# Second attention's tail reordered, and its low-rank gate computed from x in plain fp32 in four groups of 32 output partitions

## The chip, the cores and the metric

One core of a Trainium2 chip runs the kernel. The metric is the device time of one execution in microseconds (us); less is better. The core has a matrix engine (TensorE, PE in the profile), three engines for vectors (VectorE or DVE, ScalarE or ACT, GpSimd or POOL) and SyncE (SP), which only issues DMAs here. Each runs its own stream of instructions in order; they meet through semaphores.

## The reference, cut to what matters

The whole is two layers of chunked attention and retention, then a feed-forward block, a token mixer, a second feed-forward block and a norm, for 512 tokens of width 1024 in fp32. The change lies in the token mixer alone. Its input `u` is the normalised activation, and the projection `p = u @ w_in` is split into a pool part, the first linear attention ("hgrn"), the rwkv part, and the second linear attention ("gla"):

```python
gq, gk, gv, gg, ga = jnp.split(p_gla, [G, 2 * G, 3 * G, 4 * G], axis=-1)      # G = 256, ga is 16 wide
log_a = jax.nn.log_sigmoid(ga @ gla_w2 + gla_b) / GLA_GATE_TAU
o_g = chunked_gated_linear_attention(split_heads(gq * QK_SCALE), split_heads(gk),
                                     split_heads(gv), split_heads(log_a))
o_g = (o_g * lax.rsqrt(jnp.mean(o_g * o_g, axis=-1, keepdims=True) + NORM_EPS)).reshape(B, T, G)
y_gla = o_g * gla_norm * jax.nn.silu(gg)
```

The rwkv part is a recurrence over tokens with a decay `exp(-exp(w_log))`, `a = sigmoid(rwkv_a0 + xa @ rwkv_a2)`, keys normalised per head, `kk = kk / max(sqrt(sum(kk * kk)), 1e-12)`, and a gate `g_r = sigmoid(xg) @ rwkv_g2`.

## The kernel before, in words

Everything is written out by hand, one instruction stream per engine; each wait is on a named signal, and `of(name, key)` gives the value of the semaphore that the named instruction raised. The same Python loops stand in the stream of each engine, so a step `n` on one engine answers to step `n` on the others.

A weight unit is a tile of 128x1024. SyncE loads it, ScalarE rounds it to its high part (`w_high`), VectorE subtracts to get the low part (`w_low`), and TensorE multiplies 8 k tiles with three passes each (high x high, high x low, low x high: 24 matmuls of 512 columns, `three_passes`). `use()` on ScalarE and VectorE splits the next unit, three units ahead. TensorE's results land in eight PSUM banks, taken in turn by `take(key, freed_by)`: it waits until what lay in that bank has been read by the instruction named at its last take. So a product can wait for a reader of eight takes ago that has nothing to do with it.

The token mixer runs in this order. Pool and hgrn projections; then `linear_attention("hgrn")`; then `linear_attention("gla")`; then `inverse` (the rwkv chunks' triangular matrices are inverted by doubling, sizes 2 to 32); then `recurrence` with the output product as its filler. A linear attention walks over nine sizes, `ORDER = (32, 16, 8, 4, 2, 1, 64, 128, 256)`. Step n is: VectorE makes the logs of the decays (`logs`), ScalarE their exponentials (`factor`), VectorE the products with keys and queries (`factors`, tile `E`), TensorE the score products (`scores`, L862 for sizes up to 64, L873 for 128, L876 for 256), and VectorE copies those (`near`, L1644) or ScalarE does (`far`). In front of the scores of each step a `fill(n + 1)` puts other work: in hgrn the four value units of hgrn, the five units "gla a", "gla q" and "gla k", then two value units of gla; in gla the other two value units and the eight rwkv projections, and from step 6 on `operand_steps`, which prepares the rwkv operands (decays, key norms, gates).

"gla a" is the low-rank gate: before, its 16 columns are padded to a unit of their own (128 output columns, three passes over the normed input `xg`), scaled by VectorE into 16 rows of `ga`, and multiplied with `gla_w2` over these 16 rows ("gla gate", 2 products of 512 columns).

What the names of the later steps stand for: "rwkv landed" (tile `shifted`) is VectorE's scaled copy of a projection, "rwkv own" ScalarE's and "rwkv mixed" VectorE's mix with the token before. "key floored" is a tiny VectorE step, "key inverse" GpSimd's power of -0.5, "key spread" ScalarE's copy of it over the key tile, "key turned" TensorE's transposes of that, "key scaled" VectorE's product. "sigma" and "a gate" are ScalarE's sigmoids of low-rank products ("sigma in", "a gate in"), "sigma summed" VectorE's scans. "mixed" is the last product of a linear attention (40 pairs of 128x64 blocks), in two halves; the second half needs "far" of size 256. `finish` norms and gates its result. `keep_busy(n)` multiplies n times 512 columns that nobody reads.

## Time and profile before

| | us |
|---|---|
| median of 3 runs | 1684.16 (1682.77 to 1685.19) |
| the profiled execution | 1687.16 |
| its span in the profile | 1685.2 |

| engine | busy us | share |
|---|---|---|
| PE (TensorE matmuls) | 1650.3 | 98% |
| DVE (VectorE) | 861.3 | 51% |
| ACT (ScalarE) | 669.0 | 40% |
| POOL (GpSimd) | 124.7 | 7% |

The mixer's part from the start of `linear_attention("hgrn")` to the end of `inverse` is about us 989 to 1235 of the span. The page's row of the granted clock of TensorE cuts the span into 40 slices of 42 us; slices 27 to 30 cover 1138 to 1264. A matmul's duration in a timeline runs until its result has landed, and the next one starts before that, so the pace of a stream is read from starts, not from durations.

### The profile page before, as it was taken

The page shows a single profiled execution, that of the slowest core. Times are in us where ns is not written, and L with a number is a line of the kernel's source. Part 1 is how long each engine was busy: PE and PEld are TensorE (multiplying, and loading weights), DVE is VectorE, ACT ScalarE, POOL GpSimd, SP SyncE. Part 2 cuts the span into 40 slices and gives each one's busy share as a digit, 9 for nine tenths or more (in the row PEclk, how much of TensorE's full clock was granted, in tenths as well). Part 3 has the DMA queues.
Part 4 walks back from the last instruction along what each step waited for, and adds up shares of the span by engine and source line. Part 5 has one row for each costly group of instructions (what it writes and reads, how often), then busy time and mean ns, then how long its engine had stood idle before and what let it go on. Part 6 is the DMA issues. An engine that isn't in the chain of part 4 may idle for free.

```text
span 1685.2 us, 23809 instructions
## 1 busy us (share of the span) xinstructions
PE 1650.3 (98%) x9540; PEld 1338.2 (79%) x9540; DVE 861.3 (51%) x1170; ACT 669.0 (40%) x1017; POOL 124.7 (7%) x126
## 2 busy tenths in 40 slices
PE   9999999999999999999999999998999999999997
PEld 6877778877777888888888878887877888888886
DVE  6733445542444565444433478577556554444333
ACT  6145565314656433233222355346333433333221
POOL 0001001000100110000000310000410200000000
PEclk9999999999999999999999999997899999999999
DMA  5412212331221223332233422220002232232331
GB/s 180 154 63 76 88 51 88 113 125 63 75 77 53 98 85 103 100 101 90 88 103 94 141 76 63 63 66 18 3 23 86 88 101 92 96 97 85 103 98 56
DMA packets 40750, 144.14 MB, mean 86 GB/s; under 512 B 4816, under 2 KB 4832, under 8 KB 40256
## 3 DMA queue, kind: packets, MB, share of 16 engines
q1 hardware_dynamic: 37296, 131.61, 24.7%
q0 software_dynamic: 2192, 8.87, 1.6%
q10 hardware_dynamic: 1152, 2.14, 0.4%
q8 instruction: 76, 1.25, 0.3%
q14 instruction: 34, 0.28, 0.1%
...
## 4 chain that ended last, share of the span: by engine, by line
PE 85%; DVE 8%; ACT 5%; issue 1%; POOL 0%; DMA 0%; DVEq 0%; ACTq 0%; SPq 0%; POOLq 0%
PE bank L497 25%; PE bank L499 24%; PE bank L498 24%; PE bank L479 3%; PE bank L1017 2%; PE bank L485 1%; DVE sb_w_low L1230 1%; PE bank L664 1%; PE bank L728 1%; PE bank L707 1%; ACT sb_w_high L1999 1%; DVE sb_E L1230 1%; PE bank L862 1%; DVE sb_near L1644 1%; DMA sb_x<-xT 0%
## 5 line engine op out<-in xcount | busy, mean ns | idle before, releaser
L1230 DVE TENSOR_TENSOR sb_w_low<-sb_raw,sb_w_high 128x1024 fp32r<-128x1024 f32 (+1 forms) x253 | 310.9, 1229 | 368.0 <-ACT sb_w_high L1999 361.5
L497 PE MATMUL bank<-sb_xg_high,sb_w_high 128*128 128x512 f32 x1176 | 465.6, 396 | 2.0 <-DVE sb_w_low L1230 1.4
L499 PE MATMUL bank<-sb_xg_high,sb_w_low 128*128 128x512 f32 x1176 | 459.0, 390 | 0.0
L498 PE MATMUL bank<-sb_xg_low,sb_w_high 128*128 128x512 f32 x1176 | 458.5, 390 | 0.0
L1999 ACT ACTIVATE sb_w_high<-sb_raw 128x1024 fp32r<-128x1024 f32 (+1 forms) x253 | 263.3, 1041 | 349.1 <-PE bank L499 325.1
L497 PEld LDWEIGHTS bank<-sb_xg_high,sb_w_high 128*128 128x128 f32 x1176 | 221.1, 188 | 65.3 <-issue 15.8
L499 PEld LDWEIGHTS bank<-sb_xg_high,sb_w_low 128*128 128x128 f32 x1176 | 221.0, 188 | 47.1
L498 PEld LDWEIGHTS bank<-sb_xg_low,sb_w_high 128*128 128x128 f32 x1176 | 221.3, 188 | 44.3 <-issue 0.2
L499 PE MATMUL bank<-sb_h_high,sb_w_low 128*128 128x512 f32 x352 | 136.9, 389 | 0.0
L497 PE MATMUL bank<-sb_h_high,sb_w_high 128*128 128x512 f32 x352 | 136.9, 389 | 0.0
L498 PE MATMUL bank<-sb_h_low,sb_w_high 128*128 128x512 f32 x352 | 136.9, 389 | 0.0
L497 PE MATMUL bank<-sb_w_high,sb_xg_high 128*128 128x512 f32 x256 | 103.2, 403 | 0.0
L498 PE MATMUL bank<-sb_w_low,sb_xg_high 128*128 128x512 f32 x256 | 100.3, 392 | 0.0
L499 PE MATMUL bank<-sb_w_high,sb_xg_low 128*128 128x512 f32 x256 | 100.0, 391 | 0.0
L2586 POOL TENSOR_TENSOR sb_square_sum<-sb_square_sum,sb_square 128x512 f32<-128x512 f32 x20 | 26.1, 1307 | 748.4 <-ACT sb_square L1999 748.4
L499 PEld LDWEIGHTS bank<-sb_h_high,sb_w_low 128*128 128x128 f32 x352 | 66.1, 188 | 13.8
L498 PEld LDWEIGHTS bank<-sb_h_low,sb_w_high 128*128 128x128 f32 x352 | 66.1, 188 | 13.8
L497 PEld LDWEIGHTS bank<-sb_h_high,sb_w_high 128*128 128x128 f32 x352 | 66.1, 188 | 13.5
L1999 ACT ACTIVATE sb_h_high<-sb_up 128x512 fp32r<-128x512 f32 x44 | 27.8, 632 | 115.8 <-DVE sb_up L1230 115.8
L1230 DVE TENSOR_TENSOR sb_up<-bank,sb_inv_rms 128x512 f32<-128x512 f32 x44 | 30.4, 691 | 78.2 <-PE bank L499 77.4
L1999 ACT ACTIVATE sb_gate<-sb_gate 128x512 f32<-128x512 f32 x44 | 27.8, 632 | 92.3 <-DVE sb_gate L1230 92.3
L497 PEld LDWEIGHTS bank<-sb_w_high,sb_xg_high 128*128 128x128 f32 x256 | 48.3, 189 | 17.1 <-issue 7.1
...
## 6 DMA issues: line engine op xcount, KB each, us to landing
...
```

The lines of the kernel that those rows point to most:

```text
L479: made = e.matmul(out, lhsT, rhs, start=n == 0, stop=n == len(pairs) - 1)
L485: made = e.transpose(banks[i][:, blk(n)], in_, mem.ident)
L497: e.matmul(out, w[0], v[0], start=first, stop=False)
L498: e.matmul(out, w[0], v[1], start=False, stop=False)
L499: return e.matmul(out, w[1], v[0], start=False, stop=last)
L664: made = e.matmul(out[k], m.feat["rk"][r, f, blk(j)], m.feat["rq"][r, f, j * P:], start=part == 0, stop=part == 1)
L707: e.matmul(out[k], m.qT[r, j, blk(q)], m.kT[r, j, 0:keys], start=True, stop=True).then_inc(*p.up("scores", n, 2 * j + k, q))
L728: made = e.matmul(out[64 * k:64 * k + 64, blk(q)], m.tok["av"][:, key, h * ATT_DIM:(h + 1) * ATT_DIM], m.probT[:, 2 * (q % 2) + k, blk(key ...
L1017: made = e.matmul(out(banks[i], t, c), left(t, c), right(t, c), start=True, stop=True)
L1230: e.tensor_tensor(out, a, b, op).then_inc(*v.up(*signal))
L1999: e.activation(out, in_, func, bias=bias, scale=scale, accum_out=accum).then_inc(*a.up(*signal))
L2586: e.tensor_tensor(out, a, b, op).then_inc(*g.up(*signal))
```

## The change

- Low-rank gate: no weight unit any more. GpSimd scales a small table `gla_w` (128 x 8 x 32, 16 columns and 16 zeros per k tile) by the norm's gain; TensorE multiplies it with `x` itself in plain fp32, k tile k into output partitions 32 (k mod 4) to 32 (k mod 4) + 31 of one bank, 8 matmuls of 512 columns. VectorE scales all 128 rows. The second product runs over 128 rows: `gla_w2` is repeated four times with zero rows between, so it sums the four partial results. This stands in the same step as "gla q" 0, the second product in the step after.
- The hgrn part's fills: one more value unit of gla takes the place of the "gla a" unit, and the gla part has one fewer.
- gla's tail: "key squares" go to a tile of their own (`key_sq`, in the room of `y_rwkv`) and to step 3, "rwkv tanh" to step 4, the gla gate's silu (`bend_gate`) to step 2 ahead of the projection's ScalarE work. `operand_steps` is cut anew; "sigma before" and its exponential go away, since `kkE` is made from the fades `eB` shifted by one token within a chunk.
- Between gla and `inverse`: "X preset" and "XT preset" are signalled per head and stand beside the two halves of "mixed"; `rE` is made after the first masks of `inverse`; gla's `finish` is cut in two, the second half behind the updates of size 2.

```diff
@@ TensorE
                 if name == "gla" and n == len(ORDER) - 1:
-                    keep_busy(3)
+                    fill(len(ORDER))
+                    keep_busy(2)
                 scores(n)
-            if name == "gla":
-                keep_busy(1)
-            fill(len(ORDER))
+            if name == "hgrn":
+                fill(len(ORDER))
...
         def gla_steps():
-            projected("gla a", 0, "gla a landed")
-            yield
-            for f in range(2):
-                i = take(("gla gate", f), ("gla sized", f))
-                p.wait_ge(*of("gla a landed"))
-                group(banks[i][:, :], [(m.gla_w2[0:16, blk(f)], m.ga[0:16, :])], "gla gate", f)
+            i = take(("gla a",), ("gla a landed",))
+            p.wait_ge(*of("gla weights"))
+            for k in range(KT):
+                r = slice(k % 4 * 32, k % 4 * 32 + 32)
+                made = e.matmul(banks[i][r, :], m.gla_w[:, k, :], x[:, k, :], start=k < 4, stop=k >= 4)
+            made.then_inc(*p.up("gla a"))
             for f in range(2):
                 projected("gla q", f, "gla q landed", f)
                 yield
+                if f == 0:
+                    for part in range(2):
+                        i = take(("gla gate", part), ("gla sized", part))
+                        p.wait_ge(*of("gla a landed"))
+                        group(banks[i][:, :], [(m.gla_w2[:, blk(part)], m.ga)], "gla gate", part)
                 projected("gla k", f, "gla k landed", f)
...
-                next(values_h if n < 3 else others if n < 8 else values_g)
+                next(values_h if n < 3 else others if n < 7 else values_g)
...
         def operand_steps():
-            yield
             for f in range(2):
                 for what, r in (("sigma", slice(0, 64)), ("a gate", slice(64, 128))):
...
-                    group(banks[i][:, at:at + 2], [(m.kI[:, f, blk(t)], mem.table("same_head")[:, 0:P:64])], "key norm")
+                    group(banks[i][:, at:at + 2], [(m.key_sq[:, f, blk(t)], mem.table("same_head")[:, 0:P:64])], "key norm")
+            yield
+            yield
+            for f in range(2):
+                i = take(("key turned", f), ("key scaled", f))
+                p.wait_ge(*of("key spread"))
+                transposes(i, [flat(m.key_sq)[:, blk(2 * t + f)] for t in range(TT)], "key turned", f)
...
             yield
             for half in range(2):
                 i = take(("gate out", half), ("g tok", half))
                 for j in range(2):
                     group(banks[i][:, j * G:(j + 1) * G], [(m.mixed[:, 7, blk(2 * half + j)], m.lora[:, 1, :])],
                           "gate out", half)
...
-            for f in range(2):
-                i = take(("key turned", f), ("key scaled", f))
-                p.wait_ge(*of("key spread"))
-                transposes(i, [flat(m.kI)[:, blk(2 * t + f)] for t in range(TT)], "key turned", f)
-            yield
-            yield
             yield
 
...
         def fill_gla(n):
             if n < 2:
-                next(values_g)
+                if n == 0:
+                    next(values_g)
                 next(projections)
@@ VectorE
                     ALU.mult, ALU.add, "rwkv mixed", f)
                 yield
 
-        rr, rk, kk, eI = m.mixed[:, 0:2, :], m.mixed[:, 2:4, :], m.bI, m.rE
+        rr, rk, kk, eI = m.mixed[:, 0:2, :], m.mixed[:, 2:4, :], m.kI, m.rE
 
         def operand_steps():
-            yield
             norms = small[:, 176:192]
             v.wait_ge(*of("key norm"))
             ts(norms, bank("key norm")[:, 0:16], 1e-24, None, ALU.max, ALU.bypass, "key floored")
             yield
-            v.wait_ge(*of("sigma", 1))
-            for f in range(2):
-                scan(m.cum[:, f, :], m.sigma[:, f, :], "sigma summed", f)
-            tt(m.tmp, m.cum, m.sigma, ALU.subtract, "sigma before")
             for f in range(2):
                 v.wait_ge(*of("key turned", f))
                 stt(kk[:, f, :], rk[:, f, :], mem.col("rwkv_k_k", f), bank("key turned", f)[:, :], ALU.mult, ALU.mult,
                     "key scaled", f)
             yield
-
+            for f in range(2):
+                v.wait_ge(*of("sigma", f))
+                scan(m.cum[:, f, :], m.sigma[:, f, :], "sigma summed", f)
+            yield
             v.wait_ge(*of("a gate", 1))
-            v.wait_ge(*of("rwkv exps"))
-            tt(m.kkE, kk, m.tmp, ALU.mult, *STEP)
             tt(m.bI, kk, m.a_gate, ALU.mult, *STEP)
-            stt(m.bI, m.bI, -1.0, eI, ALU.mult, ALU.mult, *STEP)
-            yield
             for f in range(2):
 
                 ts(m.tmp[:, f, :], m.a_gate[:, f, :], 1.0, mem.col("rwkv_k_a", f), ALU.subtract, ALU.mult, *STEP)
                 stt(rk[:, f, :], m.tmp[:, f, :], 1.0, rk[:, f, :], ALU.add, ALU.mult, *STEP)
 
-                stt(m.sigma[:, f, :], rr[:, f, :], mem.col("rwkv_r_k", f), rk[:, f, :], ALU.mult, ALU.mult, *STEP)
-            yield
-            tt(m.kI, rk, eI, ALU.mult, *STEP)
+                stt(m.sigma[:, f, :], rr[:, f, :], mem.col("rwkv_r_k", f), rk[:, f, :], ALU.mult, ALU.mult,
+                    "bonus products")
             v.wait_ge(*of("rwkv fades"))
-            tt(m.rE, rr, m.eB, ALU.mult, "rE")
+            stt(m.bI, m.bI, -1.0, eI, ALU.mult, ALU.mult, *STEP)
+            by_chunk = lambda ap: flat(ap).rearrange("p (n c) -> p n c", c=CHUNK)
+            out, keys, fades = by_chunk(m.kkE), by_chunk(kk), by_chunk(m.eB)
+            ts(out[:, :, 0:1], keys[:, :, 0:1], 1.0, None, ALU.mult, ALU.bypass, *STEP)
+            tt(out[:, :, 1:], keys[:, :, 1:], fades[:, :, 0:CHUNK - 1], ALU.mult, "kkE")
+            tt(m.kI, rk, eI, ALU.mult, "kI")
             yield
 
         projections, operand_prep = rwkv_steps(), operand_steps()
 
         def fill_gla(n):
             if n < 6:
-                if n < 2:
+                if n == 0:
                     next(values_g)
-                if n == 0:
-                    finish_hgrn()
+                    for _ in finish_hgrn():
+                        pass
                 next(projections)
                 if n in (2, 4):
...
                     next(projections)
             e.copy_predicated(chunks(ap), over_tiles(mask).bitcast(I32),
                               chunks(bank(what, h)[:, 0:TT * CHUNK])).then_inc(*v.up(*signal))
 
-        v.wait_ge(*of("X preset"))
-        v.wait_ge(*of("XT preset"))
         for h in HEADS:
             masked("AT", m.AT[:, h, :], h, mem.table("before"))
+            v.wait_ge(*of("XT preset", h))
             first_pairs("AT", m.XT[:, h, :], h, mem.chunk_pairs(1), "XT made", 2, h)
+            v.wait_ge(*of("X preset", h))
             first_pairs("X", m.X[:, h, :], h, mem.table("pairs_ts"), "X made", 2, h)
-        finish_gla()
+        tt(m.rE, m.mixed[:, 0:2, :], m.eB, ALU.mult, "rE")
+        finishing = finish_gla()
+        next(finishing)
 
...
                     update("X", m.X[:, h, :], False, h)
                 update("XT", m.XT[:, h, :], True, h)
+            if size == 2:
+                next(finishing)
             next(side, None)
@@ ScalarE
             for half in range(2):
                 a.wait_ge(*of("mixed", name, half))
+                if name == "gla" and half:
+                    preset("XT", m.XT)
                 act(m.y_tok[name][:, 2 * half:2 * half + 2, :], groups_of(bank("mixed", name, half)[:, :], G),
                     "mixed landed", name, half, scale=0.125 if name == "hgrn" else 1.0)
+                if name == "gla" and not half:
+                    a.wait_ge(*of("factors read", "gla", len(ORDER) - 1))
+                    preset("X", m.X)
...
+        def key_squares():
+            a.wait_ge(*of("rwkv mixed", 3))
+            for f in range(2):
+                act(m.key_sq[:, f, :], m.mixed[:, 2 + f, :], "key squares", func=ACT.Square, scale=mem.col("rwkv_k_k", f))
+
+        def low_rank_tanh():
+            a.wait_ge(*of("rwkv mixed", 6))
+            act(m.mixed[0:64, 6, :], m.mixed[0:64, 6, :], "rwkv tanh", func=ACT.Tanh)
+
         def operand_steps():
+            yield
+            a.wait_ge(*of("key inverse"))
+            act(heads(flat(m.key_sq)), small[:, 176:192].unsqueeze(2).to_broadcast([P, 16, 64]), "key spread")
             a.wait_ge(*of("rwkv mixed", 7))
-            act(m.mixed[0:64, 6, :], m.mixed[0:64, 6, :], "rwkv tanh", func=ACT.Tanh)
             a.wait_ge(*of("xg read", MIX_NORM))
-            for f in range(2):
-                act(m.kI[:, f, :], m.mixed[:, 2 + f, :], "key squares", func=ACT.Square, scale=mem.col("rwkv_k_k", f))
-            yield
             for f in range(2):
                 for what, out, bias in (("sigma", m.sigma, "rwkv_w0"), ("a gate", m.a_gate, "rwkv_a0")):
                     a.wait_ge(*of(what + " in", f))
                     act(out[:, f, :], bank(what, f)[:, :], what, f, func=ACT.Sigmoid, bias=mem.col(bias, f))
             act(m.mixed[:, 7, :], m.mixed[:, 7, :], "rwkv sigmoid", func=ACT.Sigmoid)
-            a.wait_ge(*of("key norm"))
-            a.wait_ge(*of("key inverse"))
-            act(heads(flat(m.kI)), small[:, 176:192].unsqueeze(2).to_broadcast([P, 16, 64]), "key spread")
+            act(small[:, 250:251], mem.ones[:, 0:1], *STEP, func=ACT.Exp)
             yield
+            yield
+            a.wait_ge(*of("sigma summed", 1))
+            act(m.rE, m.cum, "rwkv exps", func=ACT.Exp, scale=HALF_E)
+            act(m.eB, m.cum, "rwkv fades", func=ACT.Exp, scale=-HALF_E)
             for half in range(2):
                 a.wait_ge(*of("gate out", half))
                 act(m.g_tok[:, 2 * half:2 * half + 2, :], groups_of(bank("gate out", half)[:, :], G),
                     "g tok", half)
             yield
-            a.wait_ge(*of("sigma before"))
-            act(m.tmp, m.tmp, *STEP, func=ACT.Exp, scale=-HALF_E)
-            act(m.rE, m.cum, "rwkv exps", func=ACT.Exp, scale=HALF_E)
-            act(m.eB, m.cum, "rwkv fades", func=ACT.Exp, scale=-HALF_E)
-            yield
-            yield
...
         def fill_gla(n):
             if n < 2:
-                next(values_g)
                 if n == 0:
+                    next(values_g)
                     finish_hgrn()
                 next(projections)
             elif n < 6:
+                if n == 2:
+                    bend_gate("gla")
                 next(projections)
                 if n in (2, 4):
                     next(projections)
+                if n == 3:
+                    key_squares()
+                elif n == 4:
+                    low_rank_tanh()
             else:
                 next(operand_prep)
-            if n == 4:
-                bend_gate("gla")
...
             pass
-        preset("X", m.X, "factors read")
-        preset("XT", m.XT, "mixed")
         inverse(m, finish_gla)
...
                 act(out[:, i, :], bank(name, i)[:, :], name, i)
         a.wait_ge(*of("bonus in"))
         act(mem.small[:, 112:128], bank("bonus")[:, 0:16], "bonus")
-        finish_gla()
@@ GpSimd
+        g.wait_ge(s.loads("mixer tables"), 16 * 6)
+        tt(m.gla_w, m.gla_w, mem.columns(GAINS[MIX_NORM]).unsqueeze(2).to_broadcast([P, KT, 32]), ALU.mult,
+           "gla weights")
```

Left out are the room for the new tables, the same `fill_gla` on VectorE and ScalarE, and the renamed signals. Unchanged are ScalarE's "Gv" copies in `inverse`, which wait for "y made" of gla (the end of `finish`) and stand ahead of size 4's "Pm" copies, and GpSimd's `gate_steps`, whose first step behind size 2 waits for the same signal.

## Rows read from the trace of the kernel before

**Rows 1.** Windows: stretch, length, busy PE, PEld, DVE, ACT, POOL, clock, DMA share, GB/s.
```profile
1120.00:1135.00 15.00, 15.00 (x90) 12.43 (x89) 12.31 (x16) 6.54 (x7) 0.00 (x0) 1.00 0.17 52
...
1157.00:1166.00 9.00, 9.00 (x51) 7.89 (x50) 4.39 (x7) 6.99 (x10) 3.44 (x1) 0.53 0.01 2
```
**Rows 2.** Timeline of PE: start, length, what, shapes, count; plain fp32 counts two each.
```profile
1130.03 0.39 PE L499 MATMUL bank<-sb_xg_high,sb_w_low 128*128 128x512 f32 x1
1135.47 0.39 PE L499 MATMUL bank<-sb_xg_high,sb_w_low 128*128 128x512 f32 x1
...
1019.77 1.98 PE L479 MATMUL bank<-sb_ga,sb_gla_w 16*128 16x512 f32 x4
...
472.87 1.09 PE L728 MATMUL bank<-sb_probT,sb_av 128*64 128x128 f32 x16
```
**Rows 3.** Windows, just behind the second low-rank product.
```profile
1022.00:1024.00 2.00, 2.00 (x6) 1.53 (x5) 1.86 (x3) 0.43 (x1) 0.00 (x0) 0.54 0.00 0
```
**Rows 4.** Timeline of PE, the score products of two steps behind it.
```profile
1028.98 2.00 PE L862 MATMUL bank<-sb_E 64*128 64x64 f32 x32
1036.59 2.00 PE L862 MATMUL bank<-sb_E 64*128 64x64 f32 x32
```
**Rows 5.** Timeline of DVE in the gla part; in brackets idle time before, and what ended it.
```profile
1103.00 1.23 DVE L1230 TENSOR_TENSOR sb_w_low<-sb_raw,sb_w_high 128x1024 fp32r<-128x1024 f32 x1 [2.72 <-ACT sb_w_high L1999]
...
1124.47 0.69 DVE L1230 TENSOR_TENSOR sb_shifted<-bank,sb_inv_rms 128x512 f32<-128x512 f32 x1
...
1132.50 0.69 DVE L1230 TENSOR_TENSOR sb_shifted<-bank,sb_inv_rms 128x512 f32<-128x512 f32 x1
...
1142.29 1.53 DVE L1230 TENSOR_TENSOR sb_E<-sb_E,sb_kq_gla 128x1024 f32<-128x1024 f32 x1 [1.05 <-ACT sb_E L1999]
...
1144.99 0.69 DVE L1230 TENSOR_TENSOR sb_shifted<-bank,sb_inv_rms 128x512 f32<-128x512 f32 x1
```
**Rows 6.** Timeline of ACT in the gla part: value landings, a table load, the silu.
```profile
1098.97 2.85 ACT L1999 ACTIVATE sb_v_gla<-bank,sb_inv_rms_t 128x512 f32<-128x512 f32 x4
...
1137.47 1.28 ACT L1999 ACT_TABLE_LOAD   x1
1138.77 1.06 ACT L1999 ACTIVATE sb_v_gla<-sb_v_gla 128x1024 f32<-128x1024 f32 x1
```
**Rows 7.** Timelines of POOL, PE, DVE and ACT in gla's tail.
```profile
1157.88 3.44 POOL L2586 TENSOR_TENSOR sb_small<-sb_small 128x16 f32<-128x16 f32 x1 [182.54 <-DVE sb_small L1234]
...
1157.42 3.68 PE L862 MATMUL bank<-sb_E 64*128 64x64 f32 x32
...
1166.48 2.48 DVE L1250 TENSOR_TENSOR_SCAN sb_cum<-sb_mixer,sb_sigma 128x512 f32<-128x512 f32 x2
...
1161.40 1.05 ACT L1999 ACTIVATE sb_kI<-sb_small 128x1024 f32<-128x1024 f32 x1 [1.49 <-POOL sb_small L2586]
...
1165.21 1.29 ACT L1999 ACTIVATE sb_g_tok<-bank 128x512 f32<-128x512 f32 x2
...
1173.58 2.66 ACT L1999 ACTIVATE sb_far<-bank 128x512 f32<-128x512 f32 x4
...
1176.93 0.60 ACT L1999 ACTIVATE sb_y_gla<-bank 128x512 f32<-128x512 f32 x1 [0.69 <-PE bank L479]
```
**Rows 8.** Timelines of PE, DVE and POOL in the first sizes of the inverse.
```profile
1183.08 0.69 PE L1008 MATMUL bank<-sb_kkE,sb_bI 64*64 64x64 f32 x32
...
1187.46 0.42 DVE L1230 TENSOR_TENSOR sb_AT<-bank,sb_mixer 128x256 f32<-128x256 f32 x1 [4.57 <-ACT sb_XT L1999]
...
1196.95 1.06 PE L1017 MATMUL bank<-sb_Pm,sb_XT 64*64 64x32 f32 x16 [2.62 <-ACT sb_Pm L1999]
...
1199.40 0.29 DVE L1230 TENSOR_TENSOR sb_X<-sb_X,bank 128x128 f32<-128x128 f32 x1
...
1207.90 0.66 PE L1017 MATMUL bank<-sb_X,sb_CT 64*64 64x64 f32 x16
...
1203.33 2.69 POOL L2586 TENSOR_TENSOR sb_offset<-sb_tokB,sb_small 128x256 f32<-128x256 f32 x4 [0.17 <-POOL sb_CT L2586]
```

62 lines of the change are left out of this document (34 added, 28 removed).

## The prediction

> **What bounds the kernel now.** I read the page first: TensorE is busy for 98% of the span, and the row of its granted clock is full everywhere but in two slices, both in the token mixer. So the change can only pay in the mixer. Then the windows of that stretch. Up to 1143 TensorE is busy without a gap while VectorE is at 12.31 of 15 us [rows 1]: TensorE sets the pace there, with VectorE close behind. In gla's tail the clock is at its lower level (1.2 GHz): 0.53 over 1157 to 1166 [rows 1]; it fell behind the last projections, where TensorE had to wait for ScalarE's tanh. In the tail no engine is full. There a chain through all four engines decides, so I read the timelines of each engine there and followed each wait by hand. The same goes for the first sizes of the inverse, where TensorE waits 2.62 us for a copy by ScalarE and VectorE starts 4.57 us late behind "XT preset" [rows 8].
>
> All clock times below are on the scale of the trace of before. A shift of the path counts one to one on the end, because from size 4 of the inverse on the waits keep their order.
>
> **Part 1, the low-rank gate.** A weight unit takes 5.44 us of TensorE from the first to the 25th start [rows 2]. The new product is 8 plain fp32 matmuls of 512 columns. Its price one after the other comes from the second product: 2 such matmuls took 1.98 us [rows 2], four passes with a landing of 0.16 in it, so one costs 0.86 (a 512-column pass 0.43), and eight cost 6.9. But matmuls that write different groups of output partitions overlap: 8 matmuls of 128 columns into two groups of 64 took 1.09 us with the last one's landing of some 0.2 in it, where one after the other they take 8 x 0.43 / 2 = 1.72 [rows 2]. That is 0.11 each, a factor of 2 for two groups. Four groups I take at a factor of 4: 1.7 us and a landing, 1.9. The ends are 1.7 and, without any overlap, 6.9; a factor of 2 gives 3.4. The value taken is nearest to the row with groups.
>
> The Trainium skill, TensorE: Matmul & The Clock Gate, section "Measured speedup vs the span model", has three groups of 32 columns at 2.38 times, not 3. At that share four groups would give 3.2 times, an estimate of 2.2 us, and the sum below would be 0.3 higher. No row here has four groups of 32.
>
> The second product stays at two matmuls of 512 columns and 1.98 us. But behind it the clock is at 0.54 [rows 3], and the projection that follows takes from 1021.75 to the scores at 1028.98, 7.2 us, where between other steps it is 36.59 - 28.98 - 2.0 = 5.6 [rows 4]. This product used 16 rows, the idle array being the only thing that sets it apart. With 128 rows I expect the clock to stay: -1.6 us, between 0 and -1.6.
>
> One value unit takes the freed step, so the hgrn part keeps its count of units and ends 1.9 - 1.6 = **0.3 us later**. VectorE has little to do while the hgrn part's last product runs, so this shift goes on as it is. GpSimd's scaling of the table and the sixth table load are done some 25 us before TensorE asks; if not, the gap would show before "gla a".
>
> **Part 2, the gla part has one unit fewer.** TensorE saves 5.44 us, but it no longer sets the pace. VectorE's landings of two projections that have one step between them are 1132.50 - 1124.47 = 8.03 us apart [rows 5], of which 0.8 is a wait on ScalarE; TensorE needs 5.6 + 2.0 = 7.6. So VectorE's own work decides from the first landing to the last, at 1144.99 [rows 5]. Along VectorE:
> - The gla values land (2.85 us on ScalarE [rows 6]) now ahead of the root that hgrn's `finish` waits for, and VectorE's landing 0 stands behind that: +2.9 (bounds +2.5 to +3.0).
> - The removed step saves its wait and its split, 2.72 + 1.23 [rows 5], with 0.1 of issue: -4.0.
> - The silu in step 2 stands ahead of the split's first half on ScalarE: 1.28 + 1.06 [rows 6] and the 1.06 of that half, less 1.7 that VectorE has to do meanwhile: +1.7. Its old place cost 1.05 [rows 5] and a slower product, 1.53 in place of 1.23: -1.3. The squares and the tanh fit into ScalarE's waits: 0.
>
> Sum: -0.7. With part 1 the last landing comes at 1144.99 - 0.7 + 0.3 = 1144.6, **0.4 us earlier**. TensorE is done with its projections some 7 us before that: nearly the whole saved unit turns into idle time of TensorE.
>
> **Part 3, the tail.** "key floored" came at 1157.6, just before GpSimd's power of 3.44 us [rows 7]. It moves one step ahead: about 1152.0. Power to 1155.5, key spread (1.05 [rows 7]) to 1156.6, table load 1.28 [rows 6], sigma read at 1158.7. Here a bank decides: between its take for sigma 0 and its second take for the scores of size 64 TensorE takes eight, so these scores wait for ScalarE's sigma, which now stands behind the power, the spread and the table load. They start at 1158.7 instead of 1157.42 [rows 7]. They run on the lower clock, since TensorE stood idle before: 3.68 us [rows 7], to 1162.4. The transposes behind them end their first half at 1163.2, and "key scaled" begins, 7 us earlier than before (1170.3). VectorE waits from 1157.7 to 1163.2 for that. Behind it on VectorE are queued two keys, 1.6; the logs, copies and product of sizes 256 and 64, 4.4; the scans, 2.48 [rows 7] and issue: scans done at 1171.8, before 1166.48 + 2.48 = 1169.0. ScalarE: two exponentials, 2.2, then "g tok", 1.29 [rows 7], which stood ahead of the scans before, then "far", 2.66 [rows 7]: to 1178.2, where before it ended at 1176.24. The second half of "mixed" needs it and runs 1183.08 - 1176.93 = 6.15 us [rows 7, 8]. The inverse starts at 1184.4 instead of 1183.08: **+1.3**. VectorE is ready at 1181, 2 us before it was; that gain has no taker. Bounds: full clock on scores and transposes -2.5; `keep_busy` and gate product still on the lower clock when "far" is done +1.5.
>
> **Part 4, the inverse.** Let I be its start. VectorE's first mask waits for the last landing (fence), which stands behind XT preset: I + 2.6 instead of I + 4.4. That alone gains nothing, as the second pair of heads is bound by TensorE: masks end at I + 10.5 in both. Then rE, squares and sum, 3 x 1.25, instead of all of `finish`, 5.6: first update at I + 14.4, before I + 16.3 [rows 8]. ScalarE's "Pm" loses the root ahead of it: I + 12.1 instead of 1196.95 - 1183.08 = I + 13.9 [rows 8]. But the second half of `finish` (2.7 us) ends at I + 21.3, where it was at I + 16.2. On it wait ScalarE's "Gv", with size 4's "Pm" queued behind, and GpSimd's four products of 2.69 us [rows 8], with the next "below" mask (0.73) behind. TensorE's third product of size 4 needs that mask: I + 25.0, before 1207.90 - 1183.08 = I + 24.8 [rows 8]. So the head start of 1.8 is lost again: **+0.2**, between -1.7 (if TensorE keeps its clock in the transposes and VectorE's masks follow) and +3.4.
>
> **Sum.** Hgrn part +0.3, gla part -0.7, from the last landing to the start of the inverse 39.8 us instead of 38.1, which is +1.7, inverse +0.2: **+1.5**. The profiled execution took 1687.16 (span 1685.2), so it would take 1688.7; it stands 3.0 above the median of the runs, 1684.16, and against that the sum gives **1685.7**. Its own bounds, from the -2.5, +1.5, -1.7 and +3.4 above, of which no two should come in full together: 1682.5 to 1689.
>
> **Rivals.**
> A. TensorE's saving arrives whole: VectorE is not the bound in the gla part. For it: TensorE without a gap up to 1143 [rows 1]. Against: the step of 8.03 against 7.6 [rows 5, 4]. It gives -5.4 - 1.6 + 1.9 = -5.1: 1679.0.
> B. The clock holds in the tail, as sigma, norm and scores now follow the projections closer. Against: some 5 us of waiting before the scores of size 1 and again before those of size 64. It gives -2.5 in the tail and -1.5 in the inverse on top of the forecast: 1681.7.
> C. Slower: the clock falls in the inverse. TensorE waits from I + 19.3 to I + 22.7 for "Pm" behind "y made"; before, the idle time of 2.62 us [rows 8] was followed by a stretch on the lower clock. One stretch of lower clock costs about 1.7, as behind the second low-rank product (7.2 us in place of 5.6 [rows 4]), two cost 3.4. It decides if the new wait is as long as the old one. It gives 1687.4 to 1689.1; I take 1688.5.
> D. The four groups don't overlap (or two at a time): +5.0 (+1.5), since the hgrn part is bound by TensorE: 1690.7 (1687.2).
>
> **How the numbers follow.** Forecast 0.36, A 0.22, B 0.11, C 0.24, D 0.07. The measurement can tell a change of about 0.2%, 3.4 us: faster is below 1680.8, slower above 1687.5. Faster: A and a little of B, 0.23. Slower: C and D, and a little of the forecast's upper edge, 0.32. Same: 0.45. The range takes in A and D's far end: 1678.5 to 1691.0; the forecast's own is 1682.5 to 1689.
>
> **What would show it.** "gla a" as 16 rows of plain fp32 within 2 us, starts in fours; no window under 1.00 behind the second product; VectorE's last landing of a projection near 1144.6, with TensorE done by 1138; scores of size 64 starting right behind ScalarE's first sigma; "far" ending near 1178; "Gv" on ScalarE waiting for y_gla. I am wrong if VectorE waits for TensorE in the gla part, if the scores of size 64 start before sigma is read, or if "mixed" runs through without a stop.

## The result and the profile after

The changed kernel takes **1696.42 us** (median of 9 executions, 1688.46 to 1700.32), the kernel before 1686.78 beside it (9 executions, 1682.77 to 1690.96): a ratio of 1.0056, 95% interval 1.0041 to 1.0072. It is slower by 9.6 us. The forecast was 1685.7, within 1678.5 to 1691.0.

The executions of the changed kernel are of two sorts that differ in TensorE's mean granted clock: 1688.5 and 1690.2 us at 0.987, and seven between 1695.2 and 1700.3 at 0.982 to 0.984. The one with the profile is the fastest of the nine, 1688.46 (span 1686.6). Against the profiled execution of before, 1687.16, the difference is only 1.3. So this profile doesn't show one of the executions that make the median, and that has to be kept in mind in all that is read from it.

The page of the changed kernel, its span, TensorE's busy time and its clock by fortieths of the span:

```profile
span 1686.6 us, 23786 instructions
PE 1640.1 (97%) x9528; PEld 1329.2 (79%) x9528; DVE 860.0 (51%) x1169; ACT 667.3 (40%) x1016; POOL 126.5 (7%) x128
...
PEclk9999999999999999999999999996999999999998
```

The row shows the low clock in one fortieth, where gla's tail lies (the 8 in the last place is the end of the kernel). Stretches of a few us are too short to show in it.

**The low-rank gate.** The timeline of PE of the changed kernel in the hgrn part: the new product, the second product, the scores of the step behind it, which answer to [rows 2] and [rows 4]:

```profile
1011.25 1.92 PE L922 MATMUL bank<-sb_x,sb_gla_w 128*32 128x512 f32 x16
...
1020.70 1.98 PE L481 MATMUL bank<-sb_ga,sb_gla_w 128*128 128x512 f32 x4
...
1028.10 2.00 PE L864 MATMUL bank<-sb_E 64*128 64x64 f32 x32
```

Eight fp32 matmuls (16 records) in four groups take 1.92 us. Behind the second product the scores start at 1028.10, which is 5.4 us after its end in place of 7.2, and the clock stays up.

**The gla part.** VectorE's last landing of a projection, then its longest waits from 1103 to 1144, by engine and total, and in a last fence TensorE's in the same stretch to 1145:

```profile
1143.88 0.69 DVE L1239 TENSOR_TENSOR sb_shifted<-bank,sb_inv_rms 128x512 f32<-128x512 f32 x1
```

```profile
DVE sb_mixed L1247 <- ACT sb_mixed L2013: 4.8, 6, 0.8
DVE sb_w_low L1239 <- ACT sb_w_high L2013: 2.4, 3, 1.8
```

```profile
PE bank L499 <- DVE sb_w_low L1239: 0.6, 1, 0.6
```

VectorE never waits for TensorE there. TensorE, which had no gap in this stretch before, now waits 0.6 us for VectorE.

**The tail.** Timelines of DVE, POOL, ACT and PE, in that order, from the floored norms to the inverse's first product; they answer to [rows 7]:

```profile
1151.02 0.17 DVE L1243 TENSOR_SCALAR sb_small<-bank 128x16 f32<-128x16 f32 x1
...
1162.78 1.60 DVE L1247 SCALAR_TENSOR_TENSOR sb_kI<-sb_mixed,sb_cols,bank 128x512 f32<-128x512 f32 x2 [6.00 <-PE bank L487]
...
1168.87 2.55 DVE L1259 TENSOR_TENSOR_SCAN sb_cum<-sb_mixer,sb_sigma 128x512 f32<-128x512 f32 x2
...
1151.27 3.44 POOL L2608 TENSOR_TENSOR sb_small<-sb_small 128x16 f32<-128x16 f32 x1 [175.12 <-DVE sb_small L1243]
...
1157.19 0.69 ACT L2013 ACTIVATE sb_sigma<-bank,sb_cols 128x512 f32<-128x512 f32 x1
...
1171.45 1.06 ACT L2013 ACTIVATE sb_rE<-sb_cum 128x1024 f32<-128x1024 f32 x1 [2.32 <-DVE sb_cum L1259]
1172.54 1.06 ACT L2013 ACTIVATE sb_eB<-sb_cum 128x1024 f32<-128x1024 f32 x1
1173.69 1.29 ACT L2013 ACTIVATE sb_g_tok<-bank 128x512 f32<-128x512 f32 x2
1175.07 2.66 ACT L2013 ACTIVATE sb_far<-bank 128x512 f32<-128x512 f32 x4
...
1158.02 3.68 PE L864 MATMUL bank<-sb_E 64*128 64x64 f32 x32 [5.96 <-ACT sb_sigma L2013]
...
1170.30 3.20 PE L815 MATMUL bank<-sb_inv_rms,sb_ones 128*128 128x512 f32 x4
1173.43 2.00 PE L878 MATMUL bank<-sb_E 64*128 64x256 f32 x16
...
1184.43 0.69 PE L1015 MATMUL bank<-sb_kkE,sb_bI 64*64 64x64 f32 x32
```

Read it along the forecast's chain: the bank wait of the scores of size 64 on sigma (5.96 us), the low clock on them (3.68), the wait of "key scaled" (6.00), the scans, the exponentials and "g tok" ahead of far, far's end at 1177.73, the inverse at 1184.43. Each is there.

**The inverse.** Timelines of PE and ACT around size 4, which answer to [rows 8]:

```profile
1194.88 0.66 PE L1024 MATMUL bank<-sb_Pm,sb_XT 64*64 64x32 f32 x16 [0.71 <-ACT sb_Pm L2013]
...
1206.22 0.66 PE L1024 MATMUL bank<-sb_Pm,sb_XT 64*64 64x32 f32 x16 [3.45 <-ACT sb_Pm L2013]
...
1208.43 1.12 PE L1024 MATMUL bank<-sb_X,sb_CT 64*64 64x64 f32 x16 [0.97 <-POOL sb_CT L2608]
...
1204.83 0.86 ACT L2013 ACTIVATE sb_Gv<-bank 128x256 f32<-128x256 f32 x2 [4.92 <-DVE sb_y_gla L1239]
```

The wait of 2.62 us at size 2 [rows 8] has become 0.71, and a new one of 3.45 stands at size 4, behind "Gv", which waits for "y made". Behind it the clock is at its lower level for 6.8 us (from 1207.1 on).

Where do the other 8 us of the median go? That took other kernels, some of whose traces fell into executions of the second sort.

### The profile page after: what moved, and what is told of

It is laid out like the page before. It is cut to its first block, busy times and chain, and to the rows that moved or that the text cites. A ratio compares the mean times of both kernels' runs of the same rounds, so it can differ in the third digit from the quotient of the medians.

```text
span 1686.6 us, 23786 instructions
## 1 busy us (share of the span) xinstructions
PE 1640.1 (97%) x9528; PEld 1329.2 (79%) x9528; DVE 860.0 (51%) x1169; ACT 667.3 (40%) x1016; POOL 126.5 (7%) x128
## 4 chain that ended last, share of the span: by engine, by line
PE 86%; DVE 7%; ACT 4%; issue 1%; POOL 1%; DMA 0%; DVEq 0%; ACTq 0%; SPq 0%; POOLq 0%
PE bank L499 25%; PE bank L501 24%; PE bank L500 24%; PE bank L481 3%; PE bank L487 2%; PE bank L1024 1%; PE bank L666 1%; PE bank L730 1%; DVE sb_w_low L1239 1%; PE bank L709 1%; DVE sb_E L1239 1%; ACT sb_w_high L2013 1%; PE bank L864 1%; DVE sb_near L1653 0%; DMA sb_x<-xT 0%
```

## The experiments

In all of them the kernel before ran beside on the same chip; ratios are to it. The experiments are called e1 to e17, in the order in which they were made, not in that of the text. "At 0.983" is the mean granted clock of an execution. "The faster sort" and "the slower sort" are the two groups of executions above; a stretch is time that TensorE spends at 1.2 GHz without a break. Lengths and places of stretches are from the traces' record of the granted clock, and a trace shows one execution of its kernel.

### Again, and by halves

The changed kernel once more, no edit (e1):

> The changed kernel unchanged. Its nine runs fall into two groups: 1688.5 and 1690.2 us at a mean granted clock of 0.987, and 1695.2 to 1700.3 at 0.982 to 0.984, and the one execution with a trace is of the fast group. Theory K (clock): the path itself costs only +1 to +3 us, as in that trace, and most executions have further stretches at the lower clock, some 0.004 x 1690 x 2 = 13 us of them, at a place that the trace so far does not show. Then the times split in two groups again, and a trace of the slower group would show extra windows below 1.00 between the second attention and the inverse. Theory P (path): the new order of the tail waits longer in every execution, by 8 to 10 us, and the traced one was an exception; then times lie evenly between 1688 and 1700 and a trace shows later waits at full clock.

Measured: 1695.23 us (7 executions), ratio 1.0047 (1.0028 to 1.0067). Again two sorts: 1688.47, 1690.8 and 1692.05 at 0.987, four from 1695.23 to 1700.05 at 0.982 or 0.983. With the first nine that makes 5 executions of the faster sort and 11 of the slower. The trace was again of the faster sort.

Only the gate (e2: the diff's parts on `w_mix_ga`, `gla_w`, `gla_w2`, the `gla_steps` of the three engines and the fills that go with them; tail and inverse of before):

> Only the low-rank gate is changed (plain fp32 product in four groups, second product over 128 rows, one weight unit less, and the steps that move up with it); the tail and the inverse are those of before. My steps give for it: hgrn part +0.3, gla part about -0.7 to -1.3 because VectorE sets the pace, so the same as before within 1 us (ratio 0.999 to 1.000). Theory K leaves the place of the lost clock open: if it hangs on the idle time of TensorE after the projections, which this part alone makes longer, this kernel shows 1695 too. Theory P puts all of the loss in the tail, so this kernel is not slower than before (1684 to 1687).

Measured: 1685.68, ratio 1.0001 (0.9991 to 1.0010), mean clocks 0.986 to 0.990. The gate costs nothing and brings nothing that can be measured, as I had written.

Only tail and inverse (e3: the rest of the diff):

> Only the tail and the inverse are reordered; the low-rank gate is a full weight unit as before. My steps give +1.7 in the tail and +0.2 in the inverse: about 1688 to 1690 us, ratio 1.001 to 1.002, against 1686.8 before. Theory P: the whole loss is here, 1695 to 1697 (ratio 1.005 to 1.006). Theory K: in two groups by clock, or in the lower one alone if the clock is lost to the idle time that the gate part adds.

Measured: 1697.47, ratio 1.0057 (1.0038 to 1.0076); five of six executions at 0.982 to 0.984, one, 1690.95, at 0.986. The whole loss is in the tail and the inverse. This trace is of the slower sort (1696.89). The timeline of PE between the halves of 'mixed', then two windows:

```profile
1179.33 0.41 PE L480 MATMUL bank<-sb_v_gla,sb_near 128*128 128x64 f32 x2 [1.15 <-ACT sb_far L2007]
```

```profile
1178.00:1185.00 7.00, 5.85 (x38) 5.74 (x38) 4.12 (x5) 3.36 (x7) 0.00 (x0) 0.76 0.01 2
1185.00:1198.00 13.00, 13.00 (x116) 12.63 (x116) 2.63 (x6) 3.56 (x8) 1.45 (x2) 0.50 0.00 1
```

TensorE stands for 1.15 us between the halves of 'mixed', and from 1181.6 on the clock is at 1.2 GHz for 17.1 us. That covers most of the second half of 'mixed', the first products of the inverse (L1008) and its transposes; TensorE is busy without a gap in the second of the windows. The same windows of the changed kernel's own trace, where there is no such wait:

```profile
1178.00:1185.00 7.00, 7.00 (x91) 6.92 (x89) 2.77 (x4) 2.69 (x7) 0.00 (x0) 1.00 0.01 2
1185.00:1198.00 13.00, 11.94 (x304) 11.15 (x298) 9.63 (x16) 8.01 (x17) 5.18 (x6) 1.00 0.01 3
```

In 13 us, 304 matmuls against 116.

`finish` put back ahead of the first updates (e4; ScalarE's part of it goes back too, which the cut below doesn't show):

```diff
-        finishing = finish_gla()
-        next(finishing)
+        for _ in finish_gla():
+            pass
...
-            if size == 2:
-                next(finishing)
```

> The changed kernel with the second half of the last normalization (reciprocal, scaling, gate) put back ahead of the inverse's first updates on VectorE, and its root back ahead of the first copies on ScalarE, as before the change. My steps: the first update comes 1.8 us later, and the wait for Pm behind 'y made' is gone: -0.2 +- 1.5. Rival C (the clock falls in the inverse while TensorE waits behind 'y made'): this takes the cause away, so the two groups of times become one near 1687 to 1689, and windows from 1205 to 1215 us are back at 1.00.

Measured: 1692.93, ratio 1.0042 (1.0027 to 1.0058); six executions at 1688.7 to 1691.6 (0.986, 0.987), six at 1694.3 to 1701.2 (0.979 to 0.983). So the wait behind "y made" is not what parts the two sorts, and my rival C is not the missing loss. The second thing that I had written, full clock from 1205 to 1215, did not come either: there are 6.8 us at 1.2 GHz from 1204.8 on. Its trace is of the slower sort:

```profile
1170.64 1.88 PE L815 MATMUL bank<-sb_inv_rms,sb_ones 128*128 128x512 f32 x4
1172.46 2.00 PE L878 MATMUL bank<-sb_E 64*128 64x256 f32 x16
...
1178.23 0.41 PE L481 MATMUL bank<-sb_v_gla,sb_near 128*128 128x64 f32 x2 [0.96 <-ACT sb_far L2011]
```

```profile
1187.95 1.13 PE L1015 MATMUL bank<-sb_kkE,sb_bI 64*64 64x64 f32 x32
...
1200.94 0.27 PE L1024 MATMUL bank<-sb_X,sb_CT 64*64 64x64 f32 x2 [0.38 <-DVE sb_XT L1843]
```

```profile
1175.43 2.66 ACT L2011 ACTIVATE sb_far<-bank 128x512 f32<-128x512 f32 x4
```

Compare the changed kernel's trace. There the stretch at 1.2 GHz in the tail lasts 27.3 us, to 1172.9, the two fillers of `keep_busy(2)` take 3.20, and the scores behind them start at 1173.43. Here it lasts 23.9, to 1170.6, the fillers take 1.88, and the scores start at 1172.46. Far ends at the same time in both, 1177.7 and 1178.1, because ScalarE, not TensorE, sets it. So TensorE, 1 us earlier thanks to the better clock, gets 1 us to wait, and then the clock falls for 17.1 us. The inverse starts at 1187.95 in place of 1184.43.

### More and less of the wait

One filler between the halves (e5):

```diff
+                if name == "gla" and half:
+                    keep_busy(1)
                 i = take(("mixed", name, half), ("mixed landed", name, half))
```

> The changed kernel with one fp32 filler matmul of 512 columns (0.86 us at full clock) between the two halves of the last 'mixed'. In the two traces of the slower group TensorE stood still for 1.0 us at that place, waiting for ScalarE's last far copy, and the clock fell 2.7 to 3.4 us later, for 17.1 us, over the second half of 'mixed' and the start of the inverse; in the trace of the faster group the half-clock stretch before it was one slice longer, the filler ahead of it took 3.4 instead of 1.9 us, 'mixed' began 1 us later and ran through. Theory W (that wait decides): now it runs through in every execution; all times 1688 to 1690 at 0.987. Theory S (how long the earlier half-clock stretch was decides, whatever stands in 'mixed'): two groups as before, median 1695 to 1696.

Measured: 1691.37, ratio 1.0045 (1.0027 to 1.0063); eight executions at 1688.1 to 1691.9 (0.986 to 0.989), three at 1699.6 to 1701.3 (0.983). Three stayed slow, so neither forecast came out as written. In the trace, which is of the faster sort, 0.19 us of the wait is left, and the next stretch at 1.2 GHz lasts 3.4 us, from 1187.2:

```profile
1178.02 0.41 PE L481 MATMUL bank<-sb_v_gla,sb_near 128*128 128x64 f32 x2 [0.19 <-ACT sb_far L2015]
```

The fillers ahead of the last scores taken out (e6):

```diff
                     fill(len(ORDER))
-                    keep_busy(2)
```

> The changed kernel without its two filler matmuls ahead of the scores of the last size. 'mixed' then begins 1.9 us earlier, and far comes at the same time, so TensorE waits 2 to 3 us between the halves in place of 0 to 1. Theory W: all executions are of the slower group, 1695 to 1700 at 0.981 to 0.983. Theory S: the two groups stay, about one in three at 1688. Fillers that only delay: 1 us faster.

Measured: 1698.83, ratio 1.0081 (1.0068 to 1.0093); all five executions at 0.980 to 0.982. Work was left out and it became slower:

```profile
1177.82 0.69 PE L481 MATMUL bank<-sb_v_gla,sb_near 128*128 128x64 f32 x2 [2.77 <-ACT sb_far L2012]
```

The other way round, the kernel **before** given such a wait (e10):

```diff
+            for _ in range(2):
+                act(m.eB, m.cum, *STEP, func=ACT.Exp, scale=-HALF_E)
             act(m.eB, m.cum, "rwkv fades", func=ACT.Exp, scale=-HALF_E)
```

> The kernel before with ScalarE's exponential 'rwkv fades' made three times over in place of once: 2.1 us more ahead of the last far copies, so far ends near 1178.3 as in the changed kernel in place of 1176.2, and TensorE waits about 1.0 us between the halves of 'mixed'. Nothing else is changed. Theory W: that wait alone moves most executions to a mean clock of 0.983 to 0.985 with a stretch of some 17 us from 1181 on; median 1693 to 1697. By the path alone: +1.0, 1687.

Measured: 1693.00, ratio 1.0047 (1.0035 to 1.0059); all five at 0.982 to 0.984. The wait is 1.58 us, and 20.5 us at 1.2 GHz follow from 1179.4 on, where before has 3.4:

```profile
1178.88 0.43 PE L479 MATMUL bank<-sb_v_gla,sb_near 128*128 128x64 f32 x2 [1.58 <-ACT sb_far L1999]
```

One window over 'mixed' and the start of the inverse, of this kernel, then of before:

```profile
1174.00:1206.00 32.00, 28.45 (x290) 26.87 (x288) 16.48 (x25) 15.20 (x26) 3.41 (x4) 0.68 0.00 1
```

```profile
1174.00:1206.00 32.00, 29.16 (x521) 28.18 (x520) 22.08 (x37) 14.87 (x30) 7.63 (x10) 0.84 0.01 2
```

Two superfluous instructions on ScalarE, 2.1 us, cost 6.9 in all. No part of the change is in this kernel, and nothing was added to or taken from TensorE's work: only the wait is new. That is most of the loss, rebuilt.

"g tok" ahead of the exponentials, so that far comes earlier (e9):

```diff
-            a.wait_ge(*of("sigma summed", 1))
-            act(m.rE, m.cum, "rwkv exps", func=ACT.Exp, scale=HALF_E)
-            act(m.eB, m.cum, "rwkv fades", func=ACT.Exp, scale=-HALF_E)
             for half in range(2):
                 a.wait_ge(*of("gate out", half))
...
+            a.wait_ge(*of("sigma summed", 1))
+            act(m.rE, m.cum, "rwkv exps", func=ACT.Exp, scale=HALF_E)
+            act(m.eB, m.cum, "rwkv fades", func=ACT.Exp, scale=-HALF_E)
```

> The changed kernel with ScalarE's two copies 'g tok' put ahead of the two exponentials of the summed sigma, into the 2.3 us in which ScalarE waits for the scans; before, they stand behind the exponentials and ahead of the last far copies, which end at 1178.2. Theory W (a wait of about 1 us between the halves of 'mixed' lowers the clock): far ends 0.7 to 1.3 us earlier, by 1177, the second half runs through as in the kernel before (far at 1176.2, half at 1177.3), and nearly all executions are at 0.987 or above: 1686 to 1689. By the path alone, without the clock: at most -1 on each of the two groups, median 1694 to 1696.

Measured: 1691.38, ratio 1.0038 (1.0019 to 1.0056); six executions at 1685.8 to 1689.0 (0.987, 0.988), six at 1693.7 to 1700.1 (0.980 to 0.985). The faster ones are 2 to 3 us better than the changed kernel's, but half are still of the slower sort: a miss. The trace, which is of that sort, shows why:

```profile
1173.54 2.66 ACT L2013 ACTIVATE sb_far<-bank 128x512 f32<-128x512 f32 x4
```

```profile
1176.35 0.41 PE L481 MATMUL bank<-sb_v_gla,sb_near 128*128 128x64 f32 x2 [1.32 <-ACT sb_far L2013]
```

Far ends at 1176.2 as foreseen. But here the tail's stretch at 1.2 GHz lasted only 17.1 us, TensorE did the gate product at full clock and was early by still more, and the wait is 1.32.

The same with three fillers in the inverse's wait (e11):

```diff
+            if size == 2:
+                keep_busy(3)
             next(side, None)
```

> As e9, and three filler matmuls (2.6 us at full clock) in the wait of 3.45 us in which TensorE stands for Pm behind 'y made' at the inverse's size 4. If idle time is what lowers the clock there, the stretch of 6.8 us from 1207 on goes, and it is 1.5 to 3 us faster than e9: 1684 to 1687. If the filler takes a bank that is not free, or the clock falls all the same: 0 to +3 on e9.

Measured: 1697.01, ratio 1.0057 (1.0039 to 1.0074); 1685.87 and 1688.29 at 0.989, four from 1696.7 to 1697.6 at 0.984. Which sort an execution falls into is chance here, so the median of six says nothing on the filler; e15 against e14, further down, does. Its trace says something on the two sorts: up to 'mixed' this kernel is e9, word for word, but in this execution the tail's stretch lasted 23.9 us, not 17.1; TensorE came later, there is no wait between the halves, and the execution took 1685.87.

### Fillers elsewhere

Fillers in the tail's two long waits, and the one of e5 between the halves (e7; the cut shows the first two):

```diff
+                if name == "gla" and ORDER[n] in (1, 64):
+                    keep_busy(5 if ORDER[n] == 1 else 7)
```

> As the kernel with the filler between the halves of 'mixed', and fillers too in the two long waits of the tail: five matmuls (4.3 us at full clock) ahead of the scores of size 1, where TensorE stands still for 4.2 us, and seven (6.0 us) ahead of those of size 64, where it stands still for 6.0. If the idle time of TensorE is what lowers the clock, the stretch of 24 to 27 us from 1146 on goes; scores and transposes of the tail take half as long (3.7 to 1.9 us each), and the inverse starts about 1.5 to 3 us earlier: 1683 to 1687. If the fill does not keep the clock, it adds its own time, 1 to 5 us, to the changed kernel's.

Measured: 1697.09, ratio 1.0074 (1.0060 to 1.0089), at mean clocks of 0.987 to 0.990. The trace is of the slowest of the six executions, 1704.18; the others took 1695.89 to 1698.06. In it the tail's stretch has shrunk from 27.3 us to 6.8, and it cost all the same:

```profile
1146.06 4.56 PE L815 MATMUL bank<-sb_inv_rms,sb_ones 128*128 128x512 f32 x10 [0.39 <-DVE sb_shifted L1243]
1151.17 2.00 PE L864 MATMUL bank<-sb_E 64*128 64x64 f32 x32 [0.55 <-DVE sb_near L1657]
1159.37 7.68 PE L815 MATMUL bank<-sb_inv_rms,sb_ones 128*128 128x512 f32 x14 [6.20 <-ACT sb_sigma L2017]
```

The first filler works: the scores of size 1 take 2.00 us in place of 3.68. The second takes a bank that sigma's reader still holds, so it waits 6.20 us itself and then stands for 7.7 us ahead of the scores that it should have helped. A filler needs a bank as any product does. Between the halves 1.78 us of waiting are left in this trace, and 20.5 us at 1.2 GHz follow from 1186.1 on, so the kernel has lost in both ways; how much of the time goes to which was not measured.

The kernel before with four fillers ahead of the sigma products and one between the halves (e8; `keep_busy(4)` behind the first `yield` of TensorE's `operand_steps`):

> The kernel before with fillers: four matmuls (3.4 us) in its wait of 3.0 us for the tanh ahead of the sigma products, and one between the halves of 'mixed'. If idle time lowers the clock, the stretch of 17.1 us from 1148 on goes or shrinks, and sigma products and scores of size 1 take 2 x 1.8 us less: 1682 to 1684. If not: 0 to +1, 1685.6 to 1687.

Measured: 1689.56, ratio 1.0020 (1.0011 to 1.0028), at 0.987 to 0.993, which is above both of my forecasts. In its trace the first stretch in the tail has shrunk from 17.1 us to 6.8, and the inverse starts at 1186.24, 3.2 us later than before: the last scores start 0.7 us later, after a wait of 2.13 us for VectorE; they take 3.37 us in place of 2.00, for 3.4 us at 1.2 GHz now begin at 1172.3; and the filler between the halves, where before has no wait, adds its own 0.9. The time that the sigma products and the scores of size 1 gained was lost in waits for the other engines.

### The gate's clock

The gate alone (e2), with the second product over 16 of its 128 rows (e12; three quarters of the sum are left out):

```diff
-group(banks[i][:, :], [(m.gla_w2[:, blk(part)], m.ga)], "gla gate", part)
+group(banks[i][:, :], [(m.gla_w2[0:16, blk(part)], m.ga[0:16, :])], "gla gate", part)
```

> The kernel with only the low-rank gate changed, but its second product reads 16 of the 128 rows (three quarters of the sum are left out; the time is what counts). My step: 16 rows instead of 128 are what lowers the clock behind this product. Then a slice at 1.2 GHz is back at about 1020 to 1026 and costs 1 to 1.6 us there: 1686 to 1687. If it was something else (the place behind a full unit, one unit more), no slice under 1.00 from 1000 to 1100, and the same time as e2, 1685.7.

Measured: 1685.66, ratio 0.9999 (0.9990 to 1.0008). One window of this kernel, then of before, 1020 to 1027 us:

```profile
1020.00:1027.00 7.00, 7.00 (x51) 4.98 (x50) 5.13 (x7) 2.12 (x2) 0.00 (x0) 1.00 0.24 77
```

```profile
1020.00:1027.00 7.00, 7.00 (x20) 4.66 (x20) 5.46 (x7) 2.80 (x4) 0.00 (x0) 0.76 0.12 48
```

Sixteen rows and full clock. So the number of rows is not what lowered it in the kernel before. The fall near 1022 is in each of the five traces of kernels with the old gate (before, e3, e8, e10, e17) and in none of the fourteen with the new one, whatever else was edited; what of it does it stays open.

### The wait closed for good

Three fillers between the halves of the changed kernel (e13: as e5, with `keep_busy(3)`):

> The changed kernel with three filler matmuls (2.6 us at full clock) between the halves of 'mixed', more than the wait in any trace of that kernel (0 to 1.0 us). Theory W: no execution is left in the slow group; TensorE is 1 to 2.6 us late instead: 1689.5 to 1692, all at 0.986 or above. If some executions fall for another reason, about one in four stays at 1698 to 1702.

Measured: 1690.28 (1688.48 to 1691.20, 9 executions), ratio 1.0028 (1.0018 to 1.0038), all at 0.987 to 0.989. The timeline of PE between the halves; TensorE goes from the fillers into the second half without a wait:

```profile
1178.25 2.79 PE L815 MATMUL bank<-sb_inv_rms,sb_ones 128*128 128x512 f32 x6
1181.12 0.41 PE L481 MATMUL bank<-sb_v_gla,sb_near 128*128 128x64 f32 x2
```

"g tok" first, and two fillers there (e14):

> 'g tok' ahead of the exponentials, so that far ends at 1176.2, and two fillers (1.7 us) between the halves, against a wait of 1.3 us in the slow trace of that order. Theory W: one group, 1686.5 to 1689, all at 0.986 or above. Otherwise two groups as in e9 (median 1691).

Measured: 1689.58 (1688.20 to 1693.00, 8 executions), ratio 1.0024 (1.0013 to 1.0034), all at 0.986 to 0.989; 0.6 us over what I wrote.

And three fillers in the inverse as well (e15):

> As e14, with three fillers in the inverse's wait behind 'y made' too, as in e11, whose trace of the fast group has 3.4 us at 1.2 GHz there in place of 6.8. Theory W: one group, 1685.5 to 1688; at best 1 us faster than e14, so the same as before within 0.2%.

Measured: 1687.81 (1685.96 to 1691.13, 11 executions), ratio 1.0014 (1.0005 to 1.0022), all at 0.987 to 0.992; 1.8 us less than e14. The window over 'mixed' and the first sizes of the inverse, and the one over size 4:

```profile
1174.00:1206.00 32.00, 30.44 (x547) 26.40 (x545) 22.41 (x37) 15.39 (x31) 6.11 (x7) 1.00 0.01 3
1206.00:1216.00 10.00, 8.35 (x320) 8.07 (x318) 4.30 (x13) 2.61 (x8) 8.22 (x10) 1.00 0.02 3
```

In these three kernels 28 of 28 executions are of the faster sort; in the changed kernel 5 of 16. A filler does two things, though: it closes the wait, and it gives TensorE work. And these three kernels ran together, on another chip than the changed kernel's second time (e1). What leaves the wait alone as the cause is e10, which adds the wait and no work to TensorE, in a kernel without any of the change, and has five executions of five in the slower sort, where the kernel before beside it, on the same chip as e1, has none of 23.

The changed kernel's and e11's traces are of the faster sort, and the waits of their slower executions were not seen; those of e3, e4 and e9, which share the tail, were. The traces side by side (the wait is in the PE timeline between the halves of 'mixed', the stretch is the one at 1.2 GHz that begins between 1174 and 1193 us; the last column counts the executions with a mean clock of at most 0.985, the slower sort):

| kernel | wait, us | stretch at 1.2 GHz, us | slower sort |
|---|---|---|---|
| changed, its two traces | none | none | 11 of 16 |
| e11 | none | none | 4 of 6 |
| e13, e15, e2 | none | none | 0 of 32 |
| e14 | none | 3.4 | 0 of 8 |
| before, e8, e12, e16, e17 | none | 3.4 | 0 of 43, without before's own |
| e5 | 0.19 | 3.4 | 3 of 11 |
| e4 | 0.96 | 17.1 | 6 of 12 |
| e3 | 1.15 | 17.1 | 5 of 6 |
| e9 | 1.32 | 17.1 | 6 of 12 |
| e10 | 1.58 | 20.5 | 5 of 5 |
| e7 | 1.78 | 20.5 | 0 of 6 by the clock, but all take 1695.9 or more |
| e6 | 2.77 | 23.9 | 5 of 5 |

### The smaller fall: three fillers in the inverse's first wait

Three fillers in the inverse's first wait (2.62 us [rows 8]), in the kernel with the new gate alone (e16) and in the kernel before (e17):

```diff
             product(0)
             product(1)
+            if size == 2:
+                keep_busy(3)
```

> Only the low-rank gate changed (as e2, the same time as before), and three filler matmuls (2.6 us at full clock) in the inverse's wait of 2.6 us for the first Pm of size 2. Theory: the wait lowers the clock there, so the 6.8 us at 1.2 GHz from 1196 to 1203 go; of its 6.2 us of matmuls TensorE saves up to 3, less what VectorE then bounds: 1.5 to 2.5 us faster than e2 and before, 1683 to 1684. If the filler does not keep the clock or takes a bank that is not free: 0 to +2.

> The kernel before with the same three fillers in the same wait. Theory: as e16, 1683 to 1684, ratio 0.998 to 0.999; the gate's change adds nothing to it.

Measured, in the same order: e16 1684.95, ratio 0.9994 (0.9985 to 1.0003); e17 **1683.92** (11 executions) against 1686.25, ratio 0.9990 (0.9980 to 1.0000). One window of e17, then of before:

```profile
1195.00:1204.00 9.00, 8.97 (x230) 7.08 (x227) 7.61 (x14) 3.94 (x9) 5.85 (x7) 1.00 0.02 5
```

```profile
1195.00:1204.00 9.00, 7.05 (x162) 7.05 (x164) 5.68 (x10) 2.76 (x6) 3.30 (x5) 0.62 0.02 4
```

The 6.8 us at 1.2 GHz behind the wait are gone in both kernels' traces. e17 came out as forecast and has the lowest median of all kernels here; but its interval ends at 1.0000, and e16, 1 us over its forecast, is the same as before. That the filler makes the kernel faster is likely, not shown.

## Why the prediction was right and wrong

**Part 1** (+0.3 us): price right, balance not. The new product takes 1.92 us against 1.9, and the second one 1.98. But the hgrn part is 0.9 earlier, not 0.3 later: the scores at 1036.59 [rows 4] stand at 1035.70. 1.8 us came back behind the second product, where I had 1.6. The other 1.1 is already there ahead of the new product (the scores before it start at 1009.12, in the trace of before at 1010.24): a short fall of the clock at 994.9 is missing in this trace. It is missing in e2's trace and there in e12's, so it is no part of the change. The reason that I gave for the gain, 128 rows in place of 16, fell with e12.

**Part 2** (last landing 0.4 us earlier): 1144.99 [rows 5] became 1143.88, 1.1 earlier, of which 0.9 came in with part 1: the gla part itself gained 0.2, not 0.7. The saved unit has turned into idle time, as the step said, and rival A is out. e2 shows it as a time: 1.0001. Of the 1.3 us that the silu's old place was to give back, the wait of 1.05 us is gone, but the slower product is still there (1.51 us).

**Part 3** (inverse at 1184.4): 1184.43. "Key floored" at 1151.02 (1152.0), sigma read at 1157.88 (1158.7), the scans done at 1171.42 (1171.8), far at 1177.73 (1178.2). In the profiled execution, though, 'mixed' ran through without a stop, for TensorE was late by the low clock itself. I had written that this would prove me wrong; the sum took the start from far's end and the second half's length, and TensorE, which set it here, happened to come at the same time. The agreement of the start is partly luck. In the executions that set the median it does stop. There the step that failed is this: "The second half of 'mixed' needs it and runs 6.15 us". I carried far's 2 us of delay through to the inverse as 1.3 us of waiting and gave the second half the duration that it had at full clock. In e4's trace it runs from 1178.23 to 1187.95, 9.7 us, where the changed kernel's own trace has 6.1, and the way from there to the first product of size 2 (X with CT) takes 13.0 us where the changed kernel's trace has 8.6 (1184.43 to 1193.02). 3.6 and 4.4 make the 8 us between the two sorts. (e3, whose tail and inverse are the changed kernel's, has 10.1 and 12.7, which makes the same.) The rows that should have warned me were among those that I quoted: behind waits of TensorE in this region its work runs on the lower clock, at 0.53 behind the tanh [rows 1] and behind "Pm" [rows 8]. I had used that for rival C, at a wait further on, and not at the wait that I had just computed.

**Part 4 and rival C.** The first product with "Pm" comes at I + 10.5, where I had 12.1, as the transposes ran at full clock. "Gv" does wait for y_gla (4.92 us), TensorE for "Pm" behind it, from I + 18.3 to I + 21.8 where I had 19.3 to 22.7, and the third product of size 4 comes at I + 24.0 instead of I + 25.0. Then 6.8 us at 1.2 GHz follow, as C has it, in a tighter part than before: by 1216.8 the shift is +2.6, and at 1240 +2.8, so the inverse cost 1.4, not 0.2. Of that 1.5 comes back at 1285, where the trace of before has 3.4 us at 1.2 GHz and this one none. C's mechanism was right and its price near; it was not what decided. What such a wait is worth is seen where it is filled: 2.3 us by the median in e17, 1.3 in e16, 1.8 in e15 against e14.

**From the profile to the median.** The sum gave 1688.7 for the profiled execution, which took 1688.46. The last line, "against that the sum gives 1685.7", took for granted that the changed kernel's median would stand as far below its profiled execution as the one of before did (3.0, from three runs; against 24 later runs of before it would have been 1.6). It stood 8.0 above. These two, 3.0 and 8.0, less the 0.2 by which the sum was too high, are the 10.7 us between forecast and measurement. A sum made along one trace holds for executions that go like that trace.

The Trainium skill (TensorE: Matmul & The Clock Gate, section "A second HAM failure mode: psum-queue depth-cycling") describes a kernel in which frequent short idle times between groups of matmuls make the clock swing, and puts the cost into the falls and returns between bursts. The traces here agree that short idle time can do it, and here a single wait did: 0.96 us in e4, followed by 17.1 us at 1.2 GHz. The rule of thumb in its section "Why this matters for your kernels", which warns of idle gaps much longer than that, would have let this wait pass. My estimate of 2.2 us for the gate's product, scaled from its figure for three groups of columns (section "Measured speedup vs the span model"), was too careful: 1.92.
